# Attention scores on half the rows of TensorE: two tiles of a differential head in one group, and banded heads two at a time

## The reference

```python
# banded: WINDOW = 128, group g of 4 query heads shares key head h, head_dim 64
s = einsum('bnqhgd,bnshd->bnhgqs', qb, kk) * (d ** -0.5)     # keys: own block of 128 and the one before
s = where(band & valid_blk, s, -inf)
p = softmax(concatenate([s, sink], -1))[..., :-1]
out = einsum('bnhgqs,bnshd->bnqhgd', p, vv)
...
# differential: 8 heads, two score maps m of head_dim 64 each, values of 128
s = einsum("bhmqd,bhmkd->bhmqk", qblk, kt) * scale + bias[None, :, None]
s = where(dist >= 0, s, -inf)
p = softmax(s, -1)
a = p[:, :, 0] - lam * p[:, :, 1]
o = rms_norm_2(einsum("bhqk,bhkd->bhqd", a, vt), subln_g) * (1.0 - lambda_init)
o = o.reshape(B, S, DIFF_WIDTH) * silu(gate)
```

## Time and profile before

| | us |
|---|---|
| median of 3 runs | 1231.56 (1230.41 to 1232.27) |
| the profiled execution, device time | 1229.82 |
| its span, first to last instruction | 1228.0 |
| TensorE matmuls busy | 1184.8 (96%) |
| weight loads into TensorE busy | 992.4 (81%) |
| VectorE busy | 857.9 (70%) |
| ScalarE busy | 598.2 (49%) |
| mean granted TensorE clock | 0.994 |

### The profile page before, as it was taken

How to read it: one execution, slowest core, us unless ns; L and a number is a source line. 1 busy time by engine, 2 the same in 40 slices (tenths; PEclk the granted TensorE clock), 3 DMA queues, 4 the chain that set the end, 5 groups by cost and what they waited for, 6 DMA issues and landing times.

```text
span 1228.0 us, 17185 instructions
## 1 busy us (share of the span) xinstructions
PE 1184.8 (96%) x6515; PEld 992.4 (81%) x6530; DVE 857.9 (70%) x1423; ACT 598.2 (49%) x1075; POOL 62.1 (5%) x62
## 2 busy tenths in 40 slices
PE   5999899998899999999999999999999999999998
PEld 5899788886789897777777777888887888788898
DVE  5886666758858335788888895699777687763351
ACT  6644364535546446665676655322655323652230
POOL 3029200000000000000000000000000000000001
PEclk9999999999999999999999999999999999999999
DMA  9956221110155421222212223332221432323221
GB/s 360 376 207 210 86 68 54 52 52 18 35 173 169 158 85 37 84 72 86 69 36 86 69 69 138 103 103 86 86 71 57 148 102 75 112 89 102 85 88 52
DMA packets 34002, 129.19 MB, mean 105 GB/s; under 512 B 3968, under 2 KB 4224, under 8 KB 33408
## 3 DMA queue, kind: packets, MB, share of 16 engines
q1 hardware_dynamic: 30384, 110.64, 27.5%
q0 software_dynamic: 3248, 17.14, 3.8%
q10 hardware_dynamic: 288, 0.31, 0.1%
HBM read 121.78 MB, written 6.29 MB: 104 GB/s over the span
## 4 chain that ended last, share of the span: by engine, by line
PE 64%; DVE 6%; ACT 3%; issue 2%; POOL 0%; DVEq 0%; ACTq 0%
PE bank L443 20%; PE bank L445 19%; PE bank L444 19%; PE bank L509 2%; PE bank L766 1%; DVE wl L1695 1%; DVE ca L2129 1%; PE bank L638 1%; PE bank L768 1%; DVE stat L2170 0%; DVE cumt L2378 0%; DVE ptl L1884 0%; ACT L1078 0%; ACT wh L1052 0%; PE bank L629 0%
## 5 line engine op out<-in xcount | busy, mean ns | idle before, releaser
L443 PE MATMUL bank<-hl,wh 128*128 128x512 f32 x880 | 360.9, 410 | 1.3 <-DVE cumt L1846 0.7
L445 PE MATMUL bank<-hh,wh 128*128 128x512 f32 x880 | 344.9, 392 | 0.0
L444 PE MATMUL bank<-hh,wl 128*128 128x512 f32 x880 | 344.0, 391 | 0.0
L1052 ACT ACTIVATE wh<-raw 128x1024 fp32r<-128x1024 f32 x185 | 191.2, 1055 | 192.5 <-PE bank L445 178.1
L1695 DVE TENSOR_TENSOR wl<-raw,wh 128x1024 fp32r<-128x1024 f32 x185 | 224.1, 1235 | 83.9 <-ACT wh L1052 83.4
L443 PEld LDWEIGHTS bank<-hl,wh 128*128 128x128 f32 x880 | 166.0, 189 | 38.3 <-issue 8.8
L445 PEld LDWEIGHTS bank<-hh,wh 128*128 128x128 f32 x880 | 165.7, 188 | 36.3
L444 PEld LDWEIGHTS bank<-hh,wl 128*128 128x128 f32 x880 | 166.3, 189 | 34.3 <-issue 4.3
L2129 DVE SCALAR_TENSOR_TENSOR ca<-u,vt,ca 128x512 f32<-128x512 f32 x232 | 157.7, 745 | 0.0
L443 PE MATMUL bank<-wl,hh 128*128 128x256 f32 (+1 forms) x352 | 100.5, 285 | 1.7 <-DVE cumt L1784 1.0
L444 PE MATMUL bank<-wh,hl 128*128 128x256 f32 (+1 forms) x352 | 99.3, 282 | 0.0
(11 more groups left out here) (316 smaller groups left out, 1851.7 us busy)
## 6 DMA issues: line engine op xcount, KB each, us to landing
raw<-in_chunks SPq DMA_DIRECT2D x193, 512.0 KB, 3.7
ada_a<-in_chunks SPq DMA_DIRECT2D x8, 512.0 KB, 12.8
ada_b<-in_chunks SPq DMA_DIRECT2D x8, 512.0 KB, 12.8
x<-in_x POOLq DMA_DIRECT2D x4, 512.0 KB, 10.8
mem_scratch<-kvm POOLq DMA_DIRECT2D x1, 2048.0 KB, 9.0
x<-in_x POOLq DMA_DIRECT2D x1, 2048.0 KB, 8.1
x_scratch<-x POOLq DMA_DIRECT2D x1, 2048.0 KB, 6.5
kvm<-mem_scratch POOLq DMA_DIRECT2D x1, 2048.0 KB, 8.4
```

The source lines that it names most:

```text
L443: pe.matmul(o, a[0], b[1], start=start, stop=False, **kw)
L444: pe.matmul(o, a[1], b[0], start=False, stop=False, **kw)
L445: return pe.matmul(o, a[0], b[0], start=False, stop=stop, **kw)
L1052: act.activation(wh[:, SLOT[nxt]], raw[:, RAW_SLOT[nxt]], ACT.Copy).then_inc(s.w_hi, 1)
```

## The change

1. *Differential scores* (`diff_scores`): called in slots 0 and 2 only, each time for two tiles. First the twelve 64-row matmuls of both tiles, into four banks, then the distances and masks of both. ScalarE's tanh of a gate moves ahead of the next head's query split. In the last head the low part of unit 27's transposed probabilities goes ahead of unit 28's normalisation, and mixing and splitting of head 6 go behind the low part of unit 31.
2. *Banded units* (`banded_scores`): unit order within four units becomes head a, head b (first two tiles), head a, head b (last two tiles); two units are scored together in every second step, with 64-row matmuls that alternate between the two heads' halves and between banks 2 and 3. Queries are split once for both heads of a chunk, over 128 partitions, into `qd` instead of the zero-padded `qz`. Row maxima and exponentials of two units follow each other; `prob` uses three rows by turns instead of two; `VALUES` and `MIX` move; the last weight splits of the stage move from step 48 to step 50 on VectorE.
3. *Start*: ScalarE's negated copy comes after the first value chunk's first copy; VectorE's two weight splits ahead of the keys' low part are left to the call behind it.
4. *Cross attention, last head*: seven taps ahead of its first normalisation become two, then the low part of unit 5, then five; the last gate moves ahead; three taps move behind the low part of unit 6.
5. *Output DMAs* are issued by SP instead of GpSimd.

```diff
-EVEN = {7: 1, 15: 2, 23: 3, 30: 4, 35: 5, 39: 6, 43: 7}
-ODD = {9: 1, 17: 2, 25: 3, 33: 4, 37: 5, 41: 6, 45: 7}
+BANDED_Q = {30: 0, 35: 1, 39: 2, 43: 3}
+BANDED_FREE = (27, 31, FOX + 3, FOX + 7)
-VALUES = {FOX + 5 + 2 * h: h for h in range(7)}
-VALUES[UNITS + 2] = 7
+VALUES = {FOX + 6 + 4 * (h // 2) + h % 2: h for h in range(6)}
+VALUES.update({UNITS + 1: 6, UNITS + 2: 7})
...
+def banded(u_):
+
+    g, r = divmod(u_ - FOX, 4)
+    return 2 * g + r % 2, r // 2
+
+
+def prob_at(u_):
+
+    return u_ % 2 if u_ < FOX else u_ % 3
...
+            def banded_scores(u_):
+
+                head, pair = banded(u_)
+                if u_ == FOX:
+                    pe.wait_ge(s.wmask_in, 32)
+                for side in range(2):
+                    banks.open(pe, 2 + side, ("S", u_ + side))
+                    pe.matmul(ps[2 + side][:], ident_b[:], wmask[:].rearrange("p a n -> p (a n)"), start=True, stop=True)
+                    if pair == 0:
+                        pe.matmul(ps[2 + side][:, 0:P], ident_b[:], masks[:, 1, :], start=False, stop=True, skip_group_check=True)
+                if pair == 0:
+                    pe.wait_ge(s.q_lo, 10 + head // 2)
+                for i in range(2):
+                    tt = 2 * pair + i
+                    q_ = slice(tt * P, tt * P + P)
+                    lo, at = max(tt - 1, 0) * P, 256 * i + (P if tt == 0 else 0)
+                    w = 256 * (i + 1) - at
+                    for q, k in ((0, 1), (1, 0), (0, 0)):
+                        for side in range(2):
+                            half = slice(HD * side, HD * side + HD)
+                            ins = pe.matmul(ps[2 + side][:, at:at + w], qd[head // 2 % 2][half, q, q_], kp0[half, k, lo:lo + w],
+                                            start=False, stop=True, skip_group_check=True)
+                            if (i, q, k) == (1, 0, 0):
+                                banks.close(ins, ("S", u_ + side))
...
-            def diff_scores(j, tt):
-                u_ = 4 * j + tt
...
+            def diff_scores(j, first):
+
+                if first == 0:
+                    pe.wait_ge(s.q_lo, Q1 + 2 * j + 2)
+                units = [(4 * j + tt, P * (tt + 1), slice(tt * P, tt * P + P)) for tt in (first, first + 1)]
+                outs = {(u_, m): ps[2 + 2 * (u_ % 2) + m][:, 0:w] for u_, w, _ in units for m in range(2)}
+                for u_, w, q_ in units:
+                    for m in range(2):
+                        banks.open(pe, 2 + 2 * (u_ % 2) + m, ("D", u_, m))
+                    for n, (q, k) in enumerate(((0, 1), (1, 0), (0, 0))):
+                        for m in range(2):
+                            half = slice(HD * m, HD * m + HD)
+                            pe.matmul(outs[u_, m], qd[j % 2][half, q, q_], kd[half, j % 2, k, 0:w], start=n == 0, stop=False)
+                for u_, w, q_ in units:
+                    for m in range(2):
+                        pe.matmul(outs[u_, m], slopes[:, j, :], dist[:, S - w:S], start=False, stop=True)
...
                     pieces(fill, at, half)
-                    diff_scores(j, tt)
+                    if tt % 2 == 0:
+                        diff_scores(j, tt)
...
+                    if (g, pair) == (0, 0):
+                        act.wait_ge(s.cum_dve, 2)
+                        act.activation(negcum[0:72, :], cum, ACT.Copy, scale=-1.0).then_inc(s.cum_hi, 1)
...
-                if 1 <= n <= UNITS:
+                if 1 <= n <= FOX:
                     exp_unit(n - 1)
+                elif n < UNITS and n % 2:
+                    exp_unit(n - 1)
+                    exp_unit(n)
...
-            banks.wait_full(dve, ("va", 1, 1))
-            ahead(("va", 3))
             banks.wait_full(dve, ("ka", 0))
             key_lo(0)
...
             for n in range(UNITS + 4):
                 key = DONE.get(n - 1)
                 kind, c = key or (None, None)
-                if 1 <= n <= UNITS:
+                if n in MIX and n > FOX + 2:
+                    window_mix(MIX[n] - 8)
+                if 1 <= n <= FOX:
                     row_max(n - 1)
+                elif n < UNITS and n % 2:
+                    row_max(n - 1)
+                    row_max(n)
```

More of the change, by code:

```diff
@@ L592, in unit_scores @@
             def unit_scores(u_):
+                if u_ >= FOX:
+                    if u_ % 2 == 0:
+                        banded_scores(u_)
+                    return
                 b = 2 + u_ % 2
[L595 to L605, removed]
-                    q_ = slice(tt * P, tt * P + P)
[L607 to L630, removed]
@@ L631, in unit_scores @@
-                banks.close(ins, ("S", u_))
+                h, tt = divmod(u_, 4)
+                c, side = divmod(h, 2)
+                if tt == 0:
+                    pe.wait_ge(s.q_lo, h + 1)
+                    banks.wait_empty(pe, ("ka", c))
+                if u_ == 0:
+                    pe.wait_ge(s.cum_done, 1)
+                    pe.wait_ge(s.sel_in, 16)
+                    pe.wait_ge(s.tables_in, 16 * 5)
+                w = P * (tt + 1)
+                q_ = slice(tt * P, tt * P + P)
@@ L658, in unit_turn @@
             def unit_turn(u_):
-                first = 0 if u_ < FOX or u_ % 2 else 1
+                first = 0 if u_ < FOX or banded(u_)[1] else 1
                 last = u_ % 4 + 1 if u_ < FOX else 4
-                turn(u_, ("PT", u_), [prob[:, u_ % 2, i * P:i * P + P] for i in range(first, last)], 5 + u_ % 2)
+                turn(u_, ("PT", u_), [prob[:, prob_at(u_), i * P:i * P + P] for i in range(first, last)], 5 + u_ % 2)
             def values_window(h):
-                banks.wait_empty(pe, ("PT", FOX + 2 * h + 1))
+                banks.wait_empty(pe, ("PT", FOX + 4 * (h // 2) + 2 + h % 2))
                 pe.wait_ge(s.v_lo, 5)
@@ L942, in _ @@
                   .then_inc(raw_loaded[RAW_SLOT[name]], 16)
+            o_view = out[0].rearrange("(t p) d -> p t d", p=P)
+            for g in range(4):
+                for pair in range(2):
+                    banks.wait_empty(sp, ("w2", g, pair))
+                    sp.dma_start(o_view[:, 2 * pair:2 * pair + 2, 256 * g:256 * g + 256],
+                                   x1r[:, 2 * pair:2 * pair + 2, 256 * g:256 * g + 256]).then_inc(s.out_sem, 16)
+            sp.wait_ge(s.out_sem, 16 * 8)
         @block.gpsimd
@@ L1959, in _ @@
                     unit_pt_lo(n - 2)
+                if n == UNITS + 2:
+                    banks.wait_full(dve, DONE[UNITS - 1])
+                    ahead(DONE[UNITS - 1])
                 if kind == "za":
```

134 lines of the change are left out of this document (72 added, 62 removed).

## The result

The changed kernel takes 1210.31 us, the median of four runs (1210.11 to 1211.13), against 1231.2 before on the same chip: a ratio of 0.9831, 95% interval 0.9814 to 0.9848. The profiled execution took 1210.5 us with a span of 1208.3, so of the span 19.7 us are gone where 14.1 were forecast.

A forecast was written before the change was run, and what follows sets the result against it. TensorE bounds the differential stage; VectorE paces the banded stage, neither engine full. Terms 3.8 + 0.9 + 7.0 + 0.8 + 1.4 + 0.2 = 14.1 us gave a 1217.5 us median, own range 1212 to 1222, wider range 1209 to 1226.

The forecast's parts named there:

- rival (b): Whole kernel: TensorE becomes the bound everywhere, 15 us more gained than forecast, 1202.5 us; chance 0.09.
- Differential heads: Up to head 6's third tile: grouped scores save 13 changes between 64-row and 128-row matmuls at 0.29, 3.8 us.
- rival (d): Differential heads: lateness exceeds its 1.3 us room, next head waits for the queries' split, 21 us slower, 1238.5; chance 0.07.
- Last head: Last differential head: saved changes and waits, 3.2 us at best, less lateness and low part; 0.9 taken (0 to 3.2).
- Banded stage: Units 34 to 46, paced by VectorE: fewer query splits and changed waits, 55.04 to 50.7 us, 4.4 less.
- queue walk: Banded units: following three engines' queues in order gave 0.5 us of waiting per group, 3.2 over six groups.
- Rival (a): Banded stage keeps its pace, new waits as large as the old; its 7.0 us go, 1224.5; chance 0.15.
- Behind it: After unit 46: unit 47's turn no longer waits, 1.6 us, and the last group gives 0.45.
- Start: Attention's start: 0.8 us less (0.2 to 4.6); a 3 us hole moves one unit later, with the clock's fall.
- Cross attention: Last head of cross attention: waits of 0.9 and 0.7 us go, 1.4 of 1.6 taken.
- The end: Output DMAs moved from GpSimd's queue to SP's: between 0.7 less and 0.6 more, 0.2 us less taken.
- (c): Change of rows costs nothing by itself, so grouping saves nothing: 3.8, 0.9 and 0.5 fall away, 1222.7; chance 0.11.

The follow-up runs named there:

- t_old: Changed kernel with only ScalarE's tanh of the gate back behind the next differential head's split of queries and keys; 1216.98 us, ratio 0.9878.
- sl: Changed kernel with VectorE's start work in TensorE's order, and the last differential head's mixing, splitting and low parts in the old order; ratio 0.9819.
- dx_old: Changed kernel with three edits undone: differential scores tile by tile, tanh in its old place, last cross-attention head in old order; 1222.18 us, ratio 0.9926.
- b_double: Changed kernel with the low part of the banded queries' split computed twice on VectorE, 0.69 us each; ratio 0.9852.
- s_order: Changed kernel with VectorE's weight splits again ahead of the keys' low part at the attention's start, ScalarE's sums still early; 1207.52 us, ratio 0.9803.
- e_pool: Changed kernel with the output's DMAs back on GpSimd's queue; ratio 0.9835, span 1209.5 us.
- b_sides: Changed kernel with two banded units' score matmuls ordered three of one head, then three of the other, per tile; ratio 0.9834.
- s_cos: Changed kernel with VectorE's start work in TensorE's order, and the rotation's cosine products moved from VectorE to GpSimd; 1207.54 us, ratio 0.9812.

## Why the prediction was right, and where its terms were off

The 1210.31 us lie in the range of 1209 to 1226, but below the forecast's own range of 1212 to 1222, on the side of rival (b), whose condition didn't come true: VectorE still paces the banded stage. (The banded terms, 4.4, 0.45, 1.6 and 0.45, make 6.9 and not 7.0, so the table's forecasts sum to 14.0.)

**Differential heads, 3.8 forecast, 5.24 measured.** The mechanism held. The price is 0.35 and not 0.29 (13 x 0.35 = 4.5): my price stopped at the slopes and left out the first matmul of the piece behind the masks. It is followed after 0.31 us in the kernel before too, and no row that I took goes that far:
```profile
592.33 0.48 PE L443 MATMUL bank<-hl,wh 128*128 128x512 f32 x1
592.64 0.40 PE L444 MATMUL bank<-hh,wl 128*128 128x512 f32 x1
```
The other 0.7 is the wait of 0.54 for ScalarE's tanh at the end of the first head (at 482.40), which an edit on ScalarE takes away and I priced at nothing. That edit matters far more than 0.7: without it the gain of the grouping is lost (t_old). The prediction asked what the grouping makes late inside a head on VectorE, found 1.3 us of room for the queries' split, and that held, rival (d) did not come. It never asked the same of ScalarE's queue, whose tanh would have been late. The result was right there by luck.

**Last head, 0.9 forecast, 0.83 measured**, by luck, since the parts differ. The new order gives 1.8 (sl). Three changes of rows should give 1.0, but dx_old, with tile by tile in the same place, takes only 0.3 more here than t_old (177.64 for 177.32), probably as VectorE sets the pace there. What takes back the rest, 1.3 to 2.0 us, no run isolates; the later scores, for which I took 0.7, are likely. The wait moved to the head's first turn.

**Banded stage, 4.4 forecast for units 34 to 46, 6.88 measured.** The pace is VectorE's (b_double), and its waits sum to the 3.2 of the queue walk, in part by luck. What was mis-sized is its work between the two points: 43.25 us where I had 45.0 (47.07 less 2.1). The splits gave their 2.0, but a further 1.9 left the window: a mixing now comes ahead of unit 34, a low part and a mixing behind unit 46, where TensorE is the bound. Small gaps are 1.7 instead of 2.5. So of the 6.88 some 3.8 is less work of VectorE between the two points and 3.1 less idle time. The pitch is 16.06, forecast 16.9. That the low clock at 320 us is gone should add nothing by itself to a stage that VectorE paces, but this wasn't tried. Rival (a) fell; rival (b) was near for the tail alone, where TensorE is now busy 10.74 of 10.74.

**Behind it, 2.05 forecast, 2.62 measured; units 32 and 33, 0.45 and 0.13.** The wait at unit 47's turn is gone, as told.

**Start, 0.8 forecast, 1.16 measured.** The moved hole is there, 2.71 us at the first turn, but not the clock's fall, in this execution. The splits were counted on the way to the row maximum, as they are. What I missed is that moving them is itself a loss: ahead of the keys VectorE now stands idle for 2.97 us, and with the splits back in that hole the stretch is 2.6 us shorter (s_order). ScalarE's early copy gives the whole gain and more. The size is uncertain by some 0.4, as the first turns of the other kernels show.

**Cross attention, 1.4 and 1.90.** Right in kind (dx_old gives 2.0). The difference is probably what a restart adds to a listed wait, seen in t_old: 1.5 of listed waits become about 2. **The end, 0.2 and 0.94**: the queue itself costs 1.0 (e_pool); I took the middle of bounds from a row of another size.

**Rivals.** (c), no price for the change of rows, is excluded by dx_old less t_old. The Trainium skill, TensorEngine Tiling (Array Packing), Key Properties, says that the engine drains at a changed tiling mode; the 0.27 us in and out agree with it, though no run separates a drain from the rest of the change. The Trainium skill, TensorEngine Tiling (Array Packing), PSUM Bottleneck, on which rival (a) stood, says that tiling doesn't speed up the emptying of PSUM, and VectorE does still pace the banded stage; yet the stage became 12.5% shorter, since the change gave VectorE another order and less work between the two points.

## What to carry to other kernels

When a change makes one engine ask for something sooner, follow each of the other engines' queues for what then comes late, ScalarE's as well as VectorE's: here one moved tanh decided whether the grouping gained 0.7 us a head or nothing (t_old). Before work is moved from one side of a wait to the other, look whether the wait still covers it; the same two splits cost nothing ahead of the keys and 2.6 us behind them. A wait in the list costs its length and a restart, here 0.44 listed and 0.7 paid.

## What was not expected of the hardware

- Six 64-row matmuls of each half of the rows take 0.91 us at a width of 256 in alternation and three by three alike (b_sides).
- A GpSimd product of 128x512 on SBUF stops VectorE for most of its 1.27 us (s_cos): 0.15 became 1.21, 0.62 became 1.53.
- The same hole of 2.7 us at the first turn left the granted clock at 1.00 in the changed kernel's profiled execution, and was followed by a fall in t_old's, as these two windows of t_old show; unit 34 then came 1.6 us later behind the first turn (142.73 against 141.13). The changed kernel's clock was 1.00 from 134 to 138 us as well. So a hole's second price is not the same in each execution.
```profile
126.00:134.00 8.00, 5.29 (x30) 4.31 (x29) 6.85 (x10) 1.11 (x5) 4.71 (x3) 1.00 0.62 197
134.00:138.00 4.00, 4.00 (x12) 3.03 (x11) 0.52 (x2) 0.08 (x1) 0.00 (x0) 0.58 0.00 0
```
